# Norm roots per token instead of per spread row, and a 48-row gate product, in a two-layer encoder trunk on one core

## What is computed

```
rms(x, g) = x * rsqrt(mean(x*x, over features) + 1e-6) * g
mod       = silu(c) @ mod_w[i] + mod_b[i]          # six vectors: shift, scale, gate, twice
h = rms(x, g0) * (1 + sc_m) + sh_m
x = x + g_m * rms(mixer(h), g1)
h = rms(x, g2) * (1 + sc_f) + sh_f
x = x + g_f * rms(conv_ffn(h), g3)
```

## Time and profile before

| | |
|---|---|
| runs | 2933.57, 2939.6, 2946.09 us, median 2939.6 |
| profiled execution | 2940.58 us |
| its span, first to last instruction | 2938.5 us |
| mean granted clock of PE | 0.968 |
| DMA, mean over the span | 216 GB/s |

### The profile page before, as it was taken

How to read it: one execution, slowest core, us unless ns; L and a number is a source line. 1 busy time by engine, 2 the same in 40 slices (tenths; PEclk the granted TensorE clock), 3 DMA queues, 4 the chain that set the end, 5 groups by cost and what they waited for, 6 DMA issues and landing times. The chain is left out here.

```text
span 2938.5 us, 57079 instructions
## 1 busy us (share of the span) xinstructions
PE 2768.2 (94%) x22010; PEld 2442.7 (83%) x22010; DVE 2094.1 (71%) x2726; ACT 1426.0 (49%) x1977; POOL 142.2 (5%) x160
## 2 busy tenths in 40 slices
PE   4599999899999999997999999998989999999998
PEld 3499998788888888885988788887878888888887
DVE  7877888888888876568865455554986666666665
ACT  2143334555555554446754333333456666664433
POOL 0000000000000000000000123120100000000000
PEclk8699999999999999998999999999989999999999
DMA  9968888778888768782655332223946566667875
GB/s 313 322 227 297 295 288 305 273 245 283 273 282 276 233 194 267 247 267 84 191 190 192 112 101 63 90 89 110 357 150 187 184 187 185 187 184 231 259 246 167
DMA packets 513063, 634.28 MB, mean 216 GB/s; under 512 B 27160, under 2 KB 451976, under 8 KB 512648
## 3 DMA queue, kind: packets, MB, share of 16 engines
q1 hardware_dynamic: 508864, 628.94, 65.7%
q10 hardware_dynamic: 4040, 3.07, 0.3%
HBM read 629.83 MB, written 2.10 MB: 215 GB/s over the span
## 5 line engine op out<-in xcount | busy, mean ns | idle before, releaser
L1290 DVE TENSOR_TENSOR wlo<-raw,whi 128x1024 fp32r<-128x1024 f32 x792 | 965.8, 1223 | 509.8 <-ACT whi L826 508.0
L826 ACT ACTIVATE whi<-raw 128x1024 fp32r<-128x1024 f32 x792 | 834.3, 1058 | 863.3 <-PE ps L2034 500.5
L2031 PE MATMUL ps<-xs,whi 128*128 128x512 f32 x3328 | 1173.9, 398 | 26.0 <-DVE xs L1716 15.0
L2034 PE MATMUL ps<-xs,wlo 128*128 128x256 f32 x3328 | 933.9, 281 | 0.0
L2031 PEld LDWEIGHTS ps<-xs,whi 128*128 128x128 f32 x3328 | 627.2, 188 | 178.3 <-issue 27.0
L2031 PE MATMUL ps<-act,whi 128*128 128x512 f32 x1920 | 676.9, 396 | 6.7 <-DVE wlo L1290 6.7
L2034 PEld LDWEIGHTS ps<-xs,wlo 128*128 128x128 f32 x3328 | 630.7, 190 | 0.0
L2034 PE MATMUL ps<-act,wlo 128*128 128x256 f32 x1920 | 539.1, 281 | 0.0
L2031 PEld LDWEIGHTS ps<-act,whi 128*128 128x128 f32 x1920 | 361.3, 188 | 90.0 <-DVE wlo L1290 8.1
L2034 PEld LDWEIGHTS ps<-act,wlo 128*128 128x128 f32 x1920 | 364.5, 190 | 0.0
L1312 DVE SCALAR_TENSOR_TENSOR macc<-raw,cact,macc 128x1024 f32<-128x1024 f32 (+1 forms) x266 | 324.5, 1220 | 12.5 <-DMA raw<-in_mod_w 6.5
(11 more groups left out here) (269 smaller groups left out, 3019.2 us busy)
## 6 DMA issues: line engine op xcount, KB each, us to landing
raw<-in_ffn_w_in SPq DMA_DIRECT2D x352, 512.0 KB, 4.3
raw<-in_mod_w SPq DMA_DIRECT2D x272, 384.0 KB, 4.6
raw<-in_mod_w SPq DMA_DIRECT2D x192, 512.0 KB, 5.8
raw<-in_ffn_w_out SPq DMA_DIRECT2D x176, 512.0 KB, 4.6
raw<-in_fox_w_in SPq DMA_DIRECT2D x96, 512.0 KB, 5.8
raw<-in_fox_w_out SPq DMA_DIRECT2D x32, 512.0 KB, 7.3
raw<-in_rwkv_w_r SPq DMA_DIRECT2D x32, 512.0 KB, 4.3
raw<-in_rwkv_w_k SPq DMA_DIRECT2D x32, 512.0 KB, 3.5
```

What stands on the lines that cost most here:

```text
L826: sc.activation(whi[:, half, :, :].rearrange("p k n -> p (k n)"), slots[slot], ACT.Copy).then_inc(w_hi, 1)
L1290: v.tensor_tensor(wlo[:, half, :, :].rearrange("p k n -> p (k n)"), slots[slot], whi[:, half, :, :].rearrange("p k n -> p (k n)").bitcast( ...
L2031: pe.matmul(ps[bank + m][:, :], whi[:, half, k, m * P:m * P + P], src[:, kt, :, :].rearrange("p u s -> p (u s)"), start=kt == 0, stop=Fals ...
L2034: last = pe.matmul(ps[bank + m][:, 0:S], wlo[:, half, k, m * P:m * P + P], src[:, kt, 0, :], start=False, stop=kt == n * PIECE_KT - 1, ski ...
```

## The change

Three things change.

The sums are taken with the squares as weights and a column of ones as moving operand, per half of the tokens: two columns of PSUM, tokens on partitions. Root and reciprocal then work on two elements per partition (`rt`). DVE multiplies the identity by each of the two columns (`rdiag`), and PE multiplies ones by this diagonal, which spreads the values to all partitions in bank 5; DVE reads `rs` there. In a projection the second half of the modulation sum is issued behind this (n < 3).

The gate's weights are laid three times beside each other (48 columns; rows 16 to 31 are only filling). Low halves stand in `nparts` rows 32 to 47, high halves in rows 0 to 15, and `gsel` selects both rows of a head at once, so one product of 48 rows replaces two of 16.

In attention a lap's modulation sum is issued in the next lap, two products behind each of the first three pieces of slab q; DVE's copy moves from hook 3 to 7. The bias is loaded by three transfers. In the first stage the rows' transposes no longer wait for the root, but the last.

```diff
+        rt = take(small, "rt", [P, TT])
+        rdiag = take(small, "rdiag", [P, TT, P])
+        rs = ps[5][:, 0:S]
...
-                sc.activation(rs[:, :], ps[3][:, 0:S], ACT.Sqrt, bias=eps[0], scale=1.0 / D).then_inc(*s["a"].inc("root"))
+                sc.activation(rt[:, :], ps[3][:, 0:TT], ACT.Sqrt, bias=eps[0], scale=1.0 / D).then_inc(*s["a"].inc("root"))
...
-            sc.dma_start(bf[:, :], a["fox_b_f"].rearrange("o h -> h o")).then_inc(fox_in, 16)
+            for n in range(3):
+                sc.dma_start(bf[HEADS * n:HEADS * n + HEADS, :], a["fox_b_f"].rearrange("o h -> h o")).then_inc(fox_in, 16)
...
-            sc.activation(wfh[:, :, :], wf[:, :, :], ACT.Copy).then_inc(*fg_a.inc("hi"))
+            sc.activation(wfh[:, :, :].rearrange("p k (c n) -> p k c n", c=3),
+                          wf[:, :, :].unsqueeze(2).broadcast_to([P, KT, 3, HEADS]), ACT.Copy).then_inc(*fg_a.inc("hi"))
...
+            def inverse_roots(steps_, spread_done):          # DVE
+                v.reciprocal(rt[:, :], rt[:, :]).then_inc(*steps_.inc("rinv"))
+                v.wait_ge(*steps_.at("rinv"))
+                for t in range(TT):
+                    v.tensor_scalar(rdiag[:, t, :], ident, rt[:, t:t + 1], None, ALU.mult).then_inc(
+                        *steps_.inc(f"rd{t}"))
+                v.wait_ge(*spread_done)
...
-                v.reciprocal(rs[:, :], rs[:, :]).then_inc(*s["v"].inc("rinv"))
-                v.wait_ge(*s["v"].at("rinv"))
+                inverse_roots(s["v"], s["pe"].at("roots"))
...
             def gate_weights():
+                v.tensor_tensor(gsel[:, :], ident[0:GATE_ROWS, 0:HEADS], ident[0:GATE_ROWS, 32:32 + HEADS],
+                                ALU.add).then_inc(*fg_v.inc("sel"))
...
-                v.tensor_tensor(neglo[:, :], negc[:, :], neghi[:, :].bitcast(F32), ALU.subtract).then_inc(
+                v.tensor_tensor(nparts[:, :], negc[:, :], neghi[:, :].bitcast(F32), ALU.subtract).then_inc(
                     *fg_v.inc("nlo"))
+                v.wait_ge(*fg_v.at("nlo"))
+                v.tensor_copy(nparts[0:HEADS, :], neghi[0:HEADS, :].bitcast(F32)).then_inc(*fg_v.inc("nparts"))
             def select(a_):
                 for h in range(2):
-                    for u, src in enumerate((neghi[:, :].bitcast(F32), neglo[:, :])):
-                        v.tensor_scalar(nsel[:, h, u, :], src, con[0:HEADS, ds(a_ * 2 + (K_ID + h), 1)], None,
-                                        ALU.mult).then_inc(*at_v.inc(f"sel{h}{u}"))
+                    v.tensor_scalar(nsel[:, h, :], nparts[:, :], gsel[:, ds(a_ * 2 + h, 1)], None,
+                                    ALU.mult).then_inc(*at_v.inc(f"sel{h}"))
...
-                    hooks[3] = lambda: adaln_out(ph_fox, i - 2)
+                    hooks[7] = lambda: adaln_out(ph_fox, i - 2)
...
+            def token_sums(bank, tile, first, end):          # PE
+                for t in range(TT):
+                    last = pe.matmul(bank[:, t:t + 1], tile[:, t * P:t * P + P], ones[:, 0:1], start=first and t == 0,
+                                     stop=end, skip_group_check=True)
+                return last
+            def inverse_roots(ready, done):
+                for t in range(TT):
+                    pe.wait_ge(*ready.at(f"rd{t}"))
+                    last = pe.matmul(ps[5][:, t * P:t * P + P], ones, rdiag[:, t, :], start=True, stop=True,
+                                     skip_group_check=True)
+                last.then_inc(*done.inc("roots"))
             def x_sum(n):
                 for t in range(KT):
-                    last = pe.matmul(ps[3][:, 0:S], ones, sq[:, t, :], start=t == 0, stop=t == KT - 1)
+                    last = token_sums(ps[3], sq[:, t, :], t == 0, t == KT - 1)
                 last.then_inc(*s["pe"].inc("sum"))
+                if n:
+                    inverse_roots(s["v"], s["pe"])
...
-                adaln_sum(ph, 1, 0)
+                adaln_sum(ph, 1, 0, 0, 2)
+                if n == 3:
+                    adaln_sum(ph, 1, 0, 1, 2)
+                inverse_roots(o["v"], o["pe"])
+                if n < 3:
+                    adaln_sum(ph, 1, 0, 1, 2)
...
-            pe.wait_ge(*norm[0]["a"].at("root"))
             for b, n in enumerate(ROW_COUNTS):
+                if b == 12:
+                    pe.wait_ge(*norm[0]["a"].at("root"))
...
-                        for u in range(2):
-                            last = pe.matmul(dst, oner[:, :], nsel[:, h, u, 0:n], start=False, stop=u == 1,
-                                             skip_group_check=True)
+                        last = pe.matmul(dst, oner[:, :], nsel[:, h, 0:n], start=False, stop=True,
+                                         skip_group_check=True)
...
-            with pe.Fori(1, 8) as i:
+            def fox_lap(i, first):
                 scores(i - 1)
-                slab(ph_fox, i - 1, 0, 4, 0, xs)
+                slab(ph_fox, i - 1, 0, 4, 0, xs,
+                     between=None if first else lambda q: adaln_sum(ph_fox, i - 2, 0, q, 3) if q < 3 else None)
...
-                adaln_sum(ph_fox, i - 1)
+            fox_lap(1, True)
+            with pe.Fori(2, 8) as i:
+                fox_lap(i, False)
```

More of the change, by code:

```diff
@@ L284, in trunk @@
         gain_out = take(small, "gain_out", [P, KT])
-        rs = take(small, "rs", [P, S])
+        rt = take(small, "rt", [P, TT])
+        rdiag = take(small, "rdiag", [P, TT, P])
         rtab = take(small, "rtab", [P, 1])
@@ L434, in trunk @@
         se_a = steps("se_a", "cexp")
-        norm = [dict(v=steps(f"norm{n}_v", ("rinv " if n == 0 else "rinv gain ") + (
+        norm = [dict(v=steps(f"norm{n}_v", ("rinv rd0 rd1 " if n == 0 else "rinv rd0 rd1 gain ") + (
                          " ".join(f"t{r}" for r in range(8)) if n == 2 else
@@ L440, in trunk @@
                      a=steps(f"norm{n}_a", "sq0 sq1 sq2 sq3 root " + " ".join(f"hi{r}" for r in range(8))),
-                     pe=steps(f"norm{n}_pe", "sum")) for n in range(4)]
+                     pe=steps(f"norm{n}_pe", "sum roots")) for n in range(4)]
         outp = [dict(a=steps(f"out{n}_a", "b sq" if n == 3 else "b sq y"), u=steps(f"out{n}_u", "u"), g=steps(f"out{n}_g", "add"),
-                     pe=steps(f"out{n}_pe", "sum"), root=steps(f"out{n}_root", "root"),
-                     v=steps(f"out{n}_v", "gain rinv t0 t1 x0 t2 x1 t3 x2 x3"))
+                     pe=steps(f"out{n}_pe", "sum roots"), root=steps(f"out{n}_root", "root"),
+                     v=steps(f"out{n}_v", "gain rinv rd0 rd1 t0 t1 x0 t2 x1 t3 x2 x3"))
                 for n in range(4)]
@@ L448, in trunk @@
         fg_a = steps("fg_a", "hi e l")
-        fg_v = steps("fg_v", "one lo z abs min ls neg nhi nlo")
+        fg_v = steps("fg_v", "one sel lo z abs min ls neg nhi nlo nparts")
         fx_a = steps("fx_a", "q k v")
         at_pe = steps("at_pe", "s t o")
-        at_v = steps("at_v", "sel00 sel01 sel10 sel11 sm0 sm1 m00 m01 m10 m11 rd d00 d01 d10 d11 p0 p1 lo0 lo1")
+        at_v = steps("at_v", "sel0 sel1 sm0 sm1 m00 m01 m10 m11 rd d00 d01 d10 d11 p0 p1 lo0 lo1")
         at_a = steps("at_a", "e00 e01 e10 e11 hi0 hi1")
@@ L901, in out_proj @@
                 sc.wait_ge(*o["pe"].at("sum"))
-                sc.activation(rs[:, :], ps[4][:, 0:S], ACT.Sqrt, bias=eps[0], scale=1.0 / D).then_inc(
+                sc.activation(rt[:, :], ps[4][:, 0:TT], ACT.Sqrt, bias=eps[0], scale=1.0 / D).then_inc(
                     *o["root"].inc("root"))
@@ L983, in _ @@
             sc.wait_ge(*fg_a.at("e"))
-            sc.activation(gb[:, :], gb[:, :], ACT.Ln, bias=con[0:HEADS, K_ONE:K_ONE + 1]).then_inc(*fg_a.inc("l"))
+            sc.activation(gb[:, :], gb[:, :], ACT.Ln, bias=con[0:GATE_ROWS, K_ONE:K_ONE + 1]).then_inc(*fg_a.inc("l"))
             early(ph_fox, 1)
@@ L1409, in residual @@
                 v.wait_ge(*o["root"].at("root"))
-                v.reciprocal(rs[:, :], rs[:, :]).then_inc(*o["v"].inc("rinv"))
-                v.wait_ge(*o["v"].at("rinv"))
+                inverse_roots(o["v"], o["pe"].at("roots"))
                 if n < 3:
@@ L1518, in gate_first @@
                 v.wait_ge(*fg_pe.at("z"))
-                v.tensor_scalar(gz[:, :], ps[3][0:HEADS, 0:S], bf[:, 0:1], None, ALU.add).then_inc(*fg_v.inc("z"))
+                v.tensor_scalar(gz[:, :], ps[3][0:GATE_ROWS, 0:S], bf[:, 0:1], None, ALU.add).then_inc(*fg_v.inc("z"))
                 v.wait_ge(*fg_v.at("z"))
@@ L2000, in _, with slab @@
         def _(pe):
-            def slab(ph, i, w0_, n, bank, src, tokens=False, ready=None, only=None, step=1):
+            def slab(ph, i, w0_, n, bank, src, tokens=False, ready=None, only=None, step=1, between=None):
                 for q in range(n) if only is None else only:
@@ L2025, in slab @@
                     last.then_inc(w_used, 1)
+                    if between:
+                        between(q)
             def paired_tile(ph, q, k, n, w, bank, src):
@@ L2101, in out_proj @@
```

(17 more changed lines are left out.)

50 lines of the change are left out of this document (27 added, 23 removed).

## The result

The changed kernel took 2966.1 us (median of four runs, 2957.9 to 2976.1) against 2936.6 us for the kernel before: a ratio of 1.010, 95% interval 1.0065 to 1.0136. The forecast was 2944, range 2925 to 2957. The profiled execution took 2959.56 us, 19.0 more than that of before, so part of the loss of 29 us between the medians isn't in the pair of traces at all.

A forecast was written before the change was run, and what follows sets the result against it. TensorE (PE), busy 94% of the span, was taken as the bound. Terms 12.4 - 1.35 + 1.8 - 0.4 + 1.8 + 5.3 - 3.5 - 12.0 = +4.0 on the median of 2939.6 gave 2944 us, range 2925 to 2957.

The forecast's parts named there:

- The sums of x: Norm sums of x: one-column products stay at 1.2 GHz, 13.7 against 9.55 us; +12.4 us for norms 1 to 3.
- The rival of the rising clock: Norms and first stage: the clock rises under the short sums, 16.6 us less, 2927 us; chance 0.17.
- Root and reciprocal: After each norm sum: root on two elements, scalings and spreading product take 2.1 instead of 2.5 us; -0.45 each, -1.35.
- Residual: Norm of the projection: DVE waits for the modulation sum's second half; +0.6 us each for n = 0 to 2, +1.8; n = 3 -0.4.
- First products behind a norm: First matmuls behind a norm: their time at clock 0.50 can last longer, 0.6 us lost each; +1.8 us.
- First stage: Start of kernel: cold sum, two more DMA issues, doubled transposes and wider low half make it later; +5.3 us.
- the rival of two more long waits: First stage: bias DMAs add two waits of about 11 us on ACT's queue; +20 to +22, 2965 us; chance 0.06.
- the 1.1 us of slack: First stage: DVE copies the columns 1.07 us after they are there, so 1.1 us was subtracted from its lateness.
- Attention: Attention laps: fewer gate products -3.5 us, and the clock holding at the turns -12.0 us.
- the same instructions, so nothing by itself: Attention: moving each lap's modulation sum into the first slab, two products behind each of three pieces, costs nothing by itself.
- half the length of every fall: Turns between attention laps: the clock then holds, so 24.0/2 comes back, -12.0 us; bounds 0 and -14.
- The rival of half the gain lost: Attention: transfers take PE's place once laps have no cold part, half of 15.5 us lost, 2951 us; chance 0.12.

The follow-up runs named there:

- Run 5: The changed kernel with dense 256-column filler products, into a bank nobody reads, around the norms of x: 2968.0 us, 1.0112 to the kernel before.
- run 4: The kernel before with only the modulation sum moved, in parts, into the next lap's first slab: 2932.6 us, 0.9984.
- run 3: The kernel before with the attention part alone (48-row gate products, moved modulation sum), norms as before: 2933.7 us, 0.9973.
- run 1: The whole change timed again, no further edit, against the kernel before: 2963.85 us (six runs), 1.0089.
- run 16: A second trace of run 3, nothing further changed: one execution, 2937.0 us.

## Why the forecast was wrong

The forecast stood 4 us above the kernel before; the pair of traces is 19 us apart. The 15 us between them, by the terms of the sum: attention +6.9, the residuals +1.8, the last norm +1.8, the first stage +1.4, the rest of layers one and two, mixer, roots and first products included, +3.1 (in which +11.3 and -9.3 stand against each other). The sums of x add 0.1.

**The sums of x** were right, and for the reason given: 13.8 us, cold from first to last, +12.5 against +12.4. Run 5 shows the price at either clock, 1.84 us for 16 instructions at 2.4 GHz and, in its last group, 3.41 at 1.2. The rival of the rising clock is refuted for such products: 64 instructions back to back, 13.8 us, raised nothing. The Trainium skill, TensorE: Matmul & The Clock Gate, Part 1, has the warm-up as a budget of time and not of matmuls; read so, these traces don't bear it out.

**Root and reciprocal**: -0.2 us a norm instead of -0.45. The step that fails is the adding up. The five terms and four hand-overs make 2.24 us and not 2.1; measured from the root's start they took 2.31, against 2.51 before. Each term was close: from the last scaling to the value in PSUM it was 1.1 us, with 0.9 to 1.1 forecast.

**Residual**: +0.9 to +1.5 a norm in the pair of traces, not +0.6; the second half of the modulation sum stood behind cold root products and took 1.71 us. For n = 3, where I wrote -0.4, the end came 1.4 us later. **First products behind a norm**: 0.9 us in all, not 1.8.

**First stage**: +6.7 against +5.3. The bias DMAs' group rose from 11.06 to 13.88 us and the causal one behind fell from 2.35 to 0.44, together the 0.9 that I took, so the rival of two more long waits is out. The step that fails is the 1.1 us of slack ahead of the copy of the columns: after the change the copy still starts 1.0 us behind the transposes, since the piece of weights that VectorE splits ahead of it (48.99 to 50.2 us) is held up by the same late root. By runs 4, 3 and 1 the first scaled tile comes at 51.6, 54.0 and 58.7 us: 2.4 from the 48 rows and their DMAs, 4.7 from the norm. In run 16, run 3 again, it came at 55.8, so these two are good to 2 us only.

Between runs 3 and 1 the norms cost 4.7 + 15.3 (output sum to scaled, three times) + 1.9 at the end, 21.9 us in their own rows, against my 19.6. That part of the sum stands.

**Attention**: -8.6 us instead of -15.5, and two steps fail. The first is "the same instructions, so nothing by itself". Over the seven laps from first to eighth scores the gate products gave 0.5 us a block, the falls went from 17 us to none (-8.5), and one of the seven modulation sums left the stretch (-1.3), 13 us together; the laps shortened by 10.9. The missing 2 to 3 us are of the size of the breaks around the cut sum, 0.3 us a lap, and of the late weights of run 4, which aren't separated. The second is that half the length of every fall was taken to come back. Behind the eighth scores a shorter block (-0.5), a fall of 3.4 instead of 6.8 us (-1.7) and the sum that moved there (+1.3) make -0.9, but the stretch grew by 2.3, all of it idle time of TensorE (5.9 us, 3.6 before): with the clock up, it comes earlier to the last pair's probabilities and waits 2.63 us for them. The rival of half the gain lost had the size; that transfers took it is shown only in so far as ACT waits for weights in run 4.

**What no term had**: this is the step that put the time outside the range; without its 12 us the kernel would have come out at 2954. The dense products, which fill most of TensorE's 94%, were taken as one fixed price at clock 1.00. They have two, 1.9% apart, and changed norms go with the dearer one in layer one: +11.3. In the pair of traces the -9.3 of layer two hid most of it. With the norms' 22, the pace's 12 and attention's -8 the change should cost 26 us; it costs 26 to 29. This sum leans on traces of single executions and supposes that layer two draws alike with either kernel, so its agreement is better than its parts.

Open: why changed norms lead to the slow pace in layer one, over stretches that begin up to three modulation sums behind the norm. That either half of the change brings it, that filler at the norms (run 5) didn't remove it, and that one product behind each modulation sum mostly did, in two traces (and two products in a third), speaks for a dependence on how the stream starts again. No run shows what in TensorE holds a pace.

## What to carry to other kernels

Short operands do not make a reduction cheap where the clock is at stake: 32 one-column products took 13.8 us at 1.2 GHz to their end, where 16 products of 256 columns took 9.3 to 10.0 and raised the clock on the way. Put such sums between dense products, where they cost their own time and 0.1 us behind each place. A clock that falls can hide a wait: look at what the engine will wait for once it is fast. Before a difference of 1% is read as the cost of an edit, cut both traces at the same events and look for it in stretches that the edit doesn't touch, and take a second trace of the same kernel.

## What was not expected of the hardware

- Two paces of one stream at a granted clock of 1.00: 346.7 and 353.3 ns a pair on average, 855 against 839 starts in 300 us, changing only at interruptions of the stream.
- The number of clock falls at one place differs between executions of one kernel: four and six in two traces of the kernel before, 24 and 41 us at 1.2 GHz.
- The clock fell while TensorE was busy 13.70 of 13.70 us, most of them with one-column products (run 5).
